# A two-layer network of fp32 products on one core: the three products of a chunk in another order, and a dozen small moves around the stages' seams

## The chip, the cores and the metric

The kernel runs on one core of one Trainium2 chip. The time is the device time of one execution in microseconds; a kernel's time is the median of its runs. TensorE is called PE here, its weight loads PEld, VectorE DVE, ScalarE ACT, GpSimd POOL, and the queue that issues most transfers SP.

## The reference, cut to what matters

Two blocks of a network of depth 2 each run after one another on x, 256 tokens of 1024 features, all in fp32. Cut to its shape:

```
for layer in 0, 1:                                    # first block
    x = x + 0.5 * swiglu(rms(x)) ;  x = x + mixer(rms(x))      # even: banded + stick-breaking attention; odd: dilated attention
    x = x + cross_attention(rms(x), rms(mem)) ; x = x + 0.5 * swiglu(rms(x))
for l in 0, 1:                                        # second block
    x = x + 0.5 * rms(swiglu(rms(x)))
    z = rms(x) @ w_in[l]                              # differential attention and an mLSTM read parts of z
    x = x + rms((g_a * (ya @ w_proj_a[l]) + g_m * (ym @ w_proj_m[l])) @ w_out[l])
    x = x + 0.5 * rms(swiglu(rms(x)))
swiglu(h) = (silu(h @ w_gate) * (h @ w_up)) @ w_down  # 1024 -> 2816 -> 1024
```

## The kernel before

There are 14 stages in a row: ffn0, even, xa0, ffn1, ffn2, odd, xa1, ffn3, ffn4, mix0, ffn5, ffn6, mix1, ffn7. Activations are held transposed, as [128 partitions, 8 chunks of features, 256 tokens]. Each fp32 product is made of three fp32r matmuls: with `w = w_hi + w_lo` and `a = hi + lo`, a chunk adds w_hi·hi, w_hi·lo and w_lo·hi. The weights come as 829 tiles of 512 KB: SP's queue loads one into `raw`, ACT casts it to `w_hi` (L1122), DVE subtracts to `w_lo` (L1558), and PE reads it from a ring of 6 slots (`RING`). A `w_tile` is 8 chunks by three matmuls of 256 columns, weights stationary, with the activations `a` or `b` moving; `down` and `tail_part` have the same three lines. A value tile (`v_half`) is the other way round: activations stationary, weights moving, and the order there is hi by w_hi, lo by w_hi, hi by w_lo. All matmuls are recorded at L476, the helper `mm`, except transposes (L879). Every third `w_tile` has a first matmul of 258 columns (`BESIDE`).

The order of work around the matmuls is written out by hand in lists of units, which each engine reads with its own part of a unit: `before(kind, layer)` stands ahead of a stage's attention, `between(kind, layer)` in it, `lstm_between(h, layer)` between the eight heads of the mLSTM. The units that the change touches are:

- `("mem",)`: ACT squares the memory's eight chunks (L1153), POOL adds them up (L2220); `("stat", "m")` is PE's sum over partitions of what POOL made.
- `vh(i, half)`: half of value tile i. `hs`, `hn`, `hb` are the three steps of a head norm: squares; their sum on PE, root on ACT (L1328) and reciprocal on DVE (L1847, then L1848, L1849); and the spread of the reciprocals over the heads by PE (`head_spread`, a matmul of 32 rows each) with DVE's products (L1873).
- `spread("diff", ...)` is such an `hb` of four matmuls and four L1873. It takes one of the two banks that `w_tile` writes in turn. DVE empties the bank of a `w_tile` at L1785.
- The stick-breaking attention (in the even stage) holds a softplus on ACT, which loads a table, between two rounds of PE.
- `post_norm` adds a normed stage to x: `temp = x * rt` is made by DVE for chunk 0 and by POOL for chunks 1 to 7 (L2335), DVE adds (L1667) and splits off the next stage's low part (L1585).
- `keep_going(n)` is n matmuls of no use, which PE runs while it waits.

The lines of a chunk in `w_tile`:

```
mm(out[:, 0:T], wh, hi[:, c, :], c == 0, False)
mm(out[:, 0:T], wh, lo[:, c, :], False, False)
last = mm(out[:, 0:T], wl, hi[:, c, :], False, c == C - 1)
```

Of the kernel before, what the change touches and what calls it, by code (L numbers as in the profile page):

```python
# [144 lines left out]
def build(nc, stream_d, x_d, mem_d, vec_d, con_d, biasa_d, biasc_d, heads_d, out_d, stages=STAGES):  # L145
    total = sum(TILES[s] for s, _ in stages)
    with ExitStack() as ctx:
# [106 lines left out]
        x_scaled = sem("x_scaled")  # L254
# [73 lines left out]
        def value_width(kind, i):  # L328
            return P if kind == "even" and i == 2 else T

        def before(kind, layer):
# [14 lines left out]
            def vh(i, half):  # L346
                return ("vh", "a" if kind == "odd" or kind == "even" else "b", "x" if kind in ("odd", "even") else "m", v, i, half, value_width(kind, i))
            if kind == "even":
                return [start(0, 1, 2), w(3, 0), hs("evq", 0, 0, 1), w(4, 1), ("col", "x"), hn("evq", 0, 0, 1),
                        hs("evq", 1, 2, 3), vh(0, 0), hn("evq", 1, 2, 3), hs("evk", 0, 4, 4), vh(0, 1), hn("evk", 0, 4, 4),  # L350
                        ("mem",), vh(1, 0), hb("evq", (0, 0, 1), (1, 2, 3)), vh(1, 1), hb("evk", (0, 4, 4)), ("stat", "m"),
                        vh(2, 0), ("col", "m"), ("att",), vh(2, 1)]
            if kind == "odd":
# [3 lines left out]
                def k(i):  # L357
# [4 lines left out]
                        w(13), hn(*q(3)), w(14), hs(*k(2)), w(15), hb("odq", q(2)[1:], q(3)[1:]), hs(*k(3)), hn(*k(2)), vh(0, 0)]  # L362
# [16 lines left out]
        def between(kind, layer):  # L379
# [3 lines left out]
            if kind == "odd":  # L383
                out = [[("vh", "a", "x", v, (g + 1) // 2, (g + 1) % 2, T)] for g in range(7)] + [[]]
                out[0].insert(0, ("hn", "odk", 3, layer, 14, 15))
                out[1].insert(0, ("hb", "odk", layer, ((2, 12, 13), (3, 14, 15))))
                return out
            if kind == "xa":
                k3 = ("xak", 3, layer, 6, 7)
                return [[("vh", "b", "m", v, 0, 1, T), ("hn", *k3)]] + [[("v", "b", "m", v, g)] for g in range(1, 4)]  # L390
# [4 lines left out]
        def lstm_between(h, layer):  # L395
# [6 lines left out]
            def spread(name, i, first):  # L402
# [4 lines left out]
                    2: [w0, spread("diff", 0, 0), w1],  # L407
                    3: [diff("hn", 2), w0, ("split", 0), ("split", 1), diff("hn", 3), w1],
                    4: [w0, spread("diff", 2, 4), long("hs", 0), w1],
# [46 lines left out]
        def _(pe):  # L456
# [25 lines left out]
            def w_tile(n, slot, out, hi, lo, ready=None, beside=0):  # L482

                wait_split(n)
                for c in range(C):
# [7 lines left out]
                    mm(out[:, 0:T], wh, lo[:, c, :], False, False)  # L493
                    last = mm(out[:, 0:T], wl, hi[:, c, :], False, c == C - 1)
# [58 lines left out]
            def v_half(buf, half, width=T):  # L553
# [9 lines left out]
                for e in range(4):  # L563
                    c = 4 * half + e
                    wh, wl = w_hi[:, slot, e * T:e * T + width], w_lo[:, slot, e * T:e * T + width]
                    for b in range(2):
                        o, tok = out[:, b * T:b * T + width], slice(b * P, b * P + P)
# [69 lines left out]
            def ffn(k, after_mixer):  # L637
# [44 lines left out]
                def down(n, slot, jj, J, first=False):  # L682
# [4 lines left out]
                    for c in range(C):  # L687
# [3 lines left out]
                        mm(out, wh, h[1][:, jj, :], False, False, True)  # L691
                        last = mm(out, wl, h[0][:, jj, :], False, False, True)
# [20 lines left out]
                if k >= 4:  # L713
                    sum_of_parts()
                    keep_going(4 if k < 7 else 0)
                t.next(x_ready, C)

            def unit(kind, *u):
# [15 lines left out]
                elif kind == "vh":  # L734
                    v_half(u[0], u[4], u[5])
# [17 lines left out]
            def head_sums(name, i, layer, a, b):  # L753
# [4 lines left out]
                if wide:  # L758
# [8 lines left out]
                if wide:  # L767
                    last = mm(bank[STAT][:, 0:T], mat, s[:, 0, :], True, True)
# [160 lines left out]
            def stick():  # L929
# [19 lines left out]
                wgt = z[:, 37:49, :].rearrange("p a t -> p (a t)").rearrange("p (h n) -> p h n", h=8)  # L949
                for h in range(8):  # L950
# [14 lines left out]
            def lstm(layer):  # L965
# [5 lines left out]
                for b in range(2):  # L971
                    last = mm(bank[1][:, 8 * b:8 * b + 8], g[:, b * P:(b + 1) * P], ident[0:8, 0:8], True, True)
                last.then_inc(gcol_mm, 1)
                pe.wait_ge(gcol_ready, t.next(gcol_ready))
# [21 lines left out]
                for h in range(8):  # L996
# [21 lines left out]
            def tail_part(tile, hi, lo, c0, c1):  # L1018
# [7 lines left out]
                for c in range(c0, c1):  # L1026
                    wh, wl = w_hi[:, slot, c * P:(c + 1) * P], w_lo[:, slot, c * P:(c + 1) * P]
                    mm(out[:, 0:T], wh, hi[:, c, :], c == 0, False)
                    mm(out[:, 0:T], wh, lo[:, c, :], False, False)
                    last = mm(out[:, 0:T], wl, hi[:, c, :], False, c == C - 1)  # L1030
# [3 lines left out]
            def mixer(kind, layer):  # L1034
# [45 lines left out]
                keep_going(4)  # L1080
# [16 lines left out]
        def _(act):  # L1097
# [75 lines left out]
            def ffn(k, following, after_mixer):  # L1173
# [25 lines left out]
                split_to(n0 + 6)  # L1199
# [1266 lines left out]
```

## Time and profile before

| what | before |
|---|---|
| runs | 2562.25, 2558.66, 2561.38 us, median 2561.38 |
| the profiled execution, its span | 2564.16 us, 2562.4 us |
| busy: PE, PEld, DVE, ACT, POOL | 2519.6, 2450.0, 1809.1, 1392.1, 241.0 us |
| matmuls, weight loads | 21289, 21289 |
| transfers | 446.43 MB, mean 174 GB/s |
| PE's granted clock, mean of the span | 0.992 |
| PE busy of the span's stretch: even (196 to 333) | 128.64 of 137 us, clock 0.93 |
| odd (795 to 900) | 102.82 of 105 us, clock 0.97 |
| mix0 (1386 to 1705), mix1 (2060 to 2381) | 314.20 of 319, 316.17 of 321 us |
| the eight ffn stretches, matmuls | 1633, 1720, 1719, 1708, 1678, 1596, 1490, 1488, together 13032 |

### The profile page before, as it was taken

To read this page: it belongs to the slowest core of one execution; us is meant where nothing else is said; L and a number is where in the kernel's file an instruction comes from. 1 tells how busy PE (TensorE), PEld (TensorE's weight loads), DVE (VectorE), ACT (ScalarE), POOL (GpSimd) and SP (SyncE) were. 2 spreads that over 40 slices of the span, in tenths; PEclk is the share of its full clock that TensorE was granted. 3 is DMA by queue.
4 is the path that set the end of the run, shared out by engine and by line. 5 is a ranking of instruction groups with operands and counts; after the bars stand their busy time and mean duration, and the time that the engine had idled before them with its cause. 6 is when DMAs were issued, how large, how long until landed. Compare 5 with 4: busy or idle time off the path is not lost.

```text
span 2562.4 us, 56110 instructions
## 1 busy us (share of the span) xinstructions
PE 2519.6 (98%) x21289; PEld 2450.0 (96%) x21289; DVE 1809.1 (71%) x2880; ACT 1392.1 (54%) x2228; POOL 241.0 (9%) x321
## 2 busy tenths in 40 slices
PE   9999999999999999999999999999999999999998
PEld 8998799999999899999999998999999999989998
DVE  7667586667667596767767767887676686687765
ACT  5445566445445766545445555654464465565543
POOL 1002011000000211000000070000000005301000
PEclk9998999999999999999999999999999999999999
DMA  7663245765655354565654543456555555435553
GB/s 268 213 198 127 96 151 159 237 209 186 200 196 172 100 175 143 193 196 172 213 190 162 191 157 120 162 171 194 192 176 193 189 164 175 139 121 177 182 195 115
DMA packets 123090, 446.43 MB, mean 174 GB/s; under 512 B 13696, under 2 KB 14848, under 8 KB 122944
## 3 DMA queue, kind: packets, MB, share of 16 engines
q1 hardware_dynamic: 120816, 436.79, 52.2%
q0 software_dynamic: 2128, 7.66, 0.9%
q8 instruction: 97, 1.59, 0.2%
q14 instruction: 49, 0.40, 0.0%
HBM read 443.34 MB, written 1.05 MB: 173 GB/s over the span
## 4 chain that ended last, share of the span: by engine, by line
PE 90%; DVE 7%; ACT 2%; issue 1%; POOL 0%; DMA 0%; SPq 0%; DVEq 0%; ACTq 0%; POOLq 0%
PE bank L476 89%; DVE w_lo L1558 2%; DVE rt L1853 1%; PE bank L879 1%; DVE z L1785 0%; DVE x L1667 0%; ACT w_hi L1122 0%; DVE rstd_x L1577 0%; DVE a L1585 0%; DVE score L1617 0%; DMA x<-in_x_dram 0%; ACT a L1143 0%; DVE score L1608 0%; DVE z L1857 0%; POOL score L2220 0%
## 5 line engine op out<-in xcount | busy, mean ns | idle before, releaser
L476 PE MATMUL bank<-a,w_hi 128*128 128x256 f32 x7472 | 1304.4, 279 | 9.9 <-ACT a L1143 4.2
L476 PEld LDWEIGHTS bank<-a,w_hi 128*128 128x128 f32 x7472 | 1132.1, 188 | 25.8 <-issue 14.4
L1558 DVE TENSOR_TENSOR w_lo<-raw,w_hi 128x1024 fp32r<-128x1024 f32 x829 | 1014.7, 1230 | 190.8 <-ACT w_hi L1122 185.4
L476 PE MATMUL bank<-a,w_lo 128*128 128x256 f32 x3736 | 1035.3, 277 | 0.0
L1122 ACT CAST w_hi<-raw 128x1024 fp32r<-128x1024 f32 x829 | 844.2, 1046 | 74.7 <-DMA raw<-in_stream_dram 51.9
L476 PE MATMUL bank<-b,w_hi 128*128 128x256 f32 (+1 forms) x4800 | 832.5, 277 | 1.2 <-DVE w_lo L1558 1.2
L476 PEld LDWEIGHTS bank<-b,w_hi 128*128 128x128 f32 x4800 | 723.9, 188 | 7.1 <-issue 3.1
L476 PEld LDWEIGHTS bank<-a,w_lo 128*128 128x128 f32 x3736 | 704.1, 188 | 0.0
L476 PE MATMUL bank<-b,w_lo 128*128 128x256 f32 x2400 | 663.5, 276 | 0.0
L476 PEld LDWEIGHTS bank<-b,w_lo 128*128 128x128 f32 x2400 | 450.9, 188 | 0.0
L1182 ACT CAST b<-hmid 128x256 fp32r<-128x256 f32 x132 | 53.7, 407 | 351.0 <-PE bank L476 335.5
L1178 ACT ACTIVATE sil<-sil 128x256 f32<-128x256 f32 x176 | 73.5, 417 | 167.2 <-DVE sil L1683 161.7
L1688 DVE TENSOR_TENSOR hmid<-bank,rstd_x 128x256 f32<-128x256 f32 x168 | 71.1, 423 | 126.3 <-PE bank L476 125.6
L1558 DVE TENSOR_TENSOR b<-hmid,b 128x256 fp32r<-128x256 f32 x132 | 56.0, 424 | 136.2 <-ACT b L1182 136.0
L476 PE MATMUL bank<-w_hi,a 128*128 128x256 f32 (+1 forms) x736 | 133.8, 285 | 0.0
L476 PEld LDWEIGHTS bank<-w_hi,a 128*128 128x128 f32 x736 | 114.7, 192 | 3.5 <-issue 2.4
L476 PE MATMUL bank<-w_lo,a 128*128 128x256 f32 (+1 forms) x368 | 103.9, 282 | 0.0
L2335 POOL TENSOR_TENSOR z<-x,rt 128x256 f32<-128x256 f32 x35 | 30.1, 894 | 642.4 <-ACT rt L1137 642.4
L1785 DVE TENSOR_TENSOR z<-bank,rstd_x 128x256 f32<-128x256 f32 x121 | 50.9, 421 | 55.8 <-PE bank L476 55.0
L1182 ACT CAST a<-hmid 128x256 fp32r<-128x256 f32 x44 | 17.9, 407 | 122.2 <-PE bank L476 117.5
L2204 POOL TENSOR_TENSOR score<-score 128x256 f32<-128x256 f32 x27 | 24.4, 903 | 610.4 <-ACT score L1153 609.6
L1702 DVE TENSOR_TENSOR hmid<-sil,hmid 128x256 f32<-128x256 f32 x176 | 74.8, 425 | 8.5 <-ACT sil L1178 0.7
(206 smaller groups left out, 1974.4 us busy)
## 6 DMA issues: line engine op xcount, KB each, us to landing
raw<-in_stream_dram SPq DMA_DIRECT2D x829, 512.0 KB, 3.8
z<-in_biasc_dram POOLq DMA_DIRECT2D x6, 512.0 KB, 4.6
z<-in_biasa_dram POOLq DMA_DIRECT2D x3, 512.0 KB, 4.9
x<-in_x_dram SPq DMA_DIRECT2D x2, 512.0 KB, 7.8
v<-in_mem_dram POOLq DMA_DIRECT2D x2, 512.0 KB, 7.0
out_dram<-x SPq DMA_DIRECT2D x8, 128.0 KB, 1.9
con<-in_con_dram POOLq DMA_DIRECT2D x1, 784.5 KB, 6.7
heads<-in_heads_dram POOLq DMA_DIRECT2D x1, 512.0 KB, 4.8
```

What stands on the lines that cost most here:

```text
L476: return nc.tensor.matmul(out, lhsT, rhs, start=start, stop=stop, skip_group_check=shared)
L879: last = nc.tensor.transpose(out[:, col:col + P], p[:, src:src + P], ident)
L1122: nc.scalar.copy(w_hi[:, slot, :], raw[:, raw_slot, :]).then_inc(hi_split, 1)
L1178: nc.scalar.activation(sil[:, jj, :], sil[:, jj, :], ACT.Silu).then_inc(silu_done, 1)
L1182: nc.scalar.copy(high_of["b"][:, to or jj, :], hmid[:, jj, :]).then_inc(hhi_done, 1)
L1558: return nc.vector.tensor_tensor(out, a, hi.bitcast(F32), ALU.subtract)
L1688: nc.vector.tensor_tensor(hmid[:, j % 2, :], gate_up_of(j, after_mixer)[1][:, 0:T], r, ALU.mult)\
L1702: nc.vector.tensor_tensor(hmid[:, jj, :], sil[:, jj, :], hmid[:, jj, :], ALU.mult)\
L1785: nc.vector.tensor_tensor(z[:, tile, :], out[:, 0:T], rstd[norm][:, :], ALU.mult).then_inc(w_evac, 1)
L1853: nc.vector.reciprocal(r, r).then_inc(hrecip, 1)
L2204: ins = nc.gpsimd.tensor_tensor(sq[:, 0, :], sq[:, 0, :], sq[:, c, :], ALU.add)
L2335: nc.gpsimd.tensor_tensor(z[:, 16 + c, :], x[:, c, :], rt[:, 0, 0:T], ALU.mult).then_inc(x_scaled, 1)
```

## The change

In `w_tile`, `down` and `tail_part` the second and third matmul of a chunk change places: high weights by high, low weights by high, high weights by low. `v_half` and the first chunks of a stage keep their orders. Beside it:

1. Even: `("mem",)` stands before the first value half; value tile 2 is computed in its full width of 256 (before: 128, the other half was of no use); 18 matmuls of no use of 128 columns stand in the stick-breaking attention before the second round, and DVE waits for them (`filled`) before its fourth output.
2. Odd: `hn(*k(3))` stands before the attention, not after its first exponentials.
3. Cross attention: the squares of `("xak", 3)` are added by a second matmul on PE instead of by POOL.
4. ffn 4 to 7: one `keep_going` matmul more ahead of `sum_of_parts()`, and 5 for 4 after it; mixers 5 for 4.
5. mLSTM: the columns of the gates go through another bank and PE waits for them later; `spread("diff", ...)` stands before w0 instead of after it at h = 2 and h = 4.
6. The mixers' `post_norm`: DVE makes all of `temp` itself.
7. Start of an ffn: DVE splits the first hidden tile before it does more scaling (`up_scale(1)`), and where x was rescaled ACT casts one more weight tile before the first silu.

```diff
@@ before(kind, layer)
             if kind == "even":
                 return [start(0, 1, 2), w(3, 0), hs("evq", 0, 0, 1), w(4, 1), ("col", "x"), hn("evq", 0, 0, 1),
-                        hs("evq", 1, 2, 3), vh(0, 0), hn("evq", 1, 2, 3), hs("evk", 0, 4, 4), vh(0, 1), hn("evk", 0, 4, 4),
-                        ("mem",), vh(1, 0), hb("evq", (0, 0, 1), (1, 2, 3)), vh(1, 1), hb("evk", (0, 4, 4)), ("stat", "m"),
+                        hs("evq", 1, 2, 3), ("mem",), vh(0, 0), hn("evq", 1, 2, 3), hs("evk", 0, 4, 4), vh(0, 1), hn("evk", 0, 4, 4),
+                        vh(1, 0), hb("evq", (0, 0, 1), (1, 2, 3)), vh(1, 1), hb("evk", (0, 4, 4)), ("stat", "m"),
                         vh(2, 0), ("col", "m"), ("att",), vh(2, 1)]
...
@@ lstm_between(h, layer)
-                    2: [w0, spread("diff", 0, 0), w1],
+                    2: [spread("diff", 0, 0), w0, w1],
...
@@ w_tile (down and tail_part alike)
-                    mm(out[:, 0:T], wh, lo[:, c, :], False, False)
-                    last = mm(out[:, 0:T], wl, hi[:, c, :], False, c == C - 1)
+                    mm(out[:, 0:T], wl, hi[:, c, :], False, False)
+                    last = mm(out[:, 0:T], wh, lo[:, c, :], False, c == C - 1)
...
@@ ffn, k >= 4
+                    keep_going(1)
                     sum_of_parts()
-                    keep_going(4 if k < 7 else 0)
+                    keep_going(5 if k < 7 else 0)
...
@@ head norm on PE
-                    last = mm(bank[STAT][:, 0:T], mat, s[:, 0, :], True, True)
+                    last = mm(bank[STAT][:, 0:T], mat, s[:, 0, :], True, added)
+                    if not added:
+                        last = mm(bank[STAT][:, 0:T], mat, s[:, 1, :], False, True)
...
@@ stick-breaking attention on PE
+                pe.wait_ge(bounded, t.next(bounded, 8) - 4)
+                for k in range(18):
+                    last = mm(bank[3][:, 384:512], ident, con[:, 0:P], False, False, True)
+                last.then_inc(filled, 1)
...
@@ lstm on PE
-                pe.wait_ge(gcol_ready, t.next(gcol_ready))
+                t.next(gcol_ready)
...
+                    if h == 0:
+                        pe.wait_ge(gcol_ready, t.so_far(gcol_ready))
...
@@ start of an ffn on ACT, then on DVE
-                split_to(n0 + 6)
+                split_to(n0 + 7 if rescaled[0] else n0 + 6)
...
-                up_scale(1, n0 + 3)
                 h_low(0, base)
                 split_to(n0 + 7)
+                up_scale(1, n0 + 3)
...
@@ post_norm on DVE; POOL's loop runs for stage "ffn" alone
+                def scaled(c):
+                    if c == 0 or not shared and c < C:
+                        chain(nc.vector.tensor_tensor(temp[:, c, :], x[:, c, :], rt[:, 0, 0:T], ALU.mult))
```

Three places as the engines' queues hold them. PE, in mix0 at h = 2, before: the end of w0 (`a` by the weights), the spread (`recip_two,spread_by`), the start of w1.

```order
L476 MATMUL bank<-a,w_lo 128x256
L476 MATMUL bank<-recip_two,spread_by 128x256 [waits w_evac,qk_ready,hrecip]
L476 MATMUL bank<-recip_two,spread_by 128x256
L476 MATMUL bank<-recip_two,spread_by 128x256 [waits h_bc]
L476 MATMUL bank<-recip_two,spread_by 128x256
L476 MATMUL bank<-a,w_hi 128x258 [waits lo_split,hi_split,w_evac]
L476 MATMUL bank<-a,w_hi 128x256
L476 MATMUL bank<-a,w_lo 128x256
```

The same place of the change: the spread, the start of w0 in the new order of a chunk (w_hi, w_lo, w_hi), and from its last matmul into w1.

```order
L472 MATMUL bank<-recip_two,spread_by 128x256 [waits h_bc]
L472 MATMUL bank<-recip_two,spread_by 128x256
L472 MATMUL bank<-a,w_hi 128x256 [waits lo_split,hi_split,w_evac]
L472 MATMUL bank<-a,w_lo 128x256
L472 MATMUL bank<-a,w_hi 128x256 x2
...
L472 MATMUL bank<-a,w_hi 128x256
L472 MATMUL bank<-a,w_hi 128x258 [waits lo_split,hi_split,qk_ready]
```

Now w1 waits for `qk_ready`, which is the last of the spread's four products on DVE, where it waited for `w_evac`, one L1785. In DVE's queue at this place, before:

```order
L2059 SCALAR_TENSOR_TENSOR v<-pt 128x256
L1785 TENSOR_TENSOR z<-bank,rstd_x 128x256 [waits tile_mm]
L1558 TENSOR_TENSOR w_lo<-raw,w_hi 128x1024 [waits hi_split]
L1873 SCALAR_TENSOR_TENSOR z<-z,vec,bank 128x256 [waits h_bc]
L1873 SCALAR_TENSOR_TENSOR z<-z,vec,bank 128x256 x3
```

and of the change, where L1883, L1795, L1563 and L2071 are before's L1873, L1785, L1558 and L2059:

```order
L2071 SCALAR_TENSOR_TENSOR v<-pt 128x256
L1883 SCALAR_TENSOR_TENSOR z<-z,vec,bank 128x256 [waits h_bc]
L1883 SCALAR_TENSOR_TENSOR z<-z,vec,bank 128x256 x3
L1795 TENSOR_TENSOR z<-bank,rstd_x 128x256 [waits tile_mm]
L1563 TENSOR_TENSOR w_lo<-raw,w_hi 128x1024 [waits hi_split]
```

The four products moved ahead of w0's L1785, and stand behind the head's own work (L2059) as before. In the odd stage DVE's queue reads before, after the first round of biases:

```order
L1558 TENSOR_TENSOR w_lo<-raw,w_hi 128x1024 [waits hi_split]
L1916 RECIPROCAL rr<-rs 128x4 [waits exp_done]
L1901 ISA score,nmx<-bank,z 128x128 [waits s_mm]
L1901 ISA nmx 128x1
L1901 ISA score,nmx<-bank,z 128x256
```

and with the change, where L1857 to L1859 are before's L1847 to L1849 (the reciprocals of `hn`), L1926 is L1916 and L1911 is L1901:

```order
L1563 TENSOR_TENSOR w_lo<-raw,w_hi 128x1024 [waits hi_split]
L1857 RECIPROCAL rt<-rt 128x256 [waits hroot]
L1858 CAST recip_two<-rt 128x256 [waits dve_step]
L1859 SCALAR_TENSOR_TENSOR recip_two<-recip_two,con,rt 128x256 [waits dve_step]
L1926 RECIPROCAL rr<-rs 128x4 [waits exp_done]
L1911 ISA score,nmx<-bank,z 128x128 [waits s_mm]
```

The three rows of `hn` moved from behind the second round of biases to ahead of L1916.

## Rows read from the trace of the kernel before

**Rows 1.** The page, busy time of each engine.

```profile
PE 2519.6 (98%) x21289; PEld 2450.0 (96%) x21289; DVE 1809.1 (71%) x2880; ACT 1392.1 (54%) x2228; POOL 241.0 (9%) x321
```

**Rows 2.** The page, costliest groups: count, busy us, mean ns of one, idle before.

```profile
L476 PE MATMUL bank<-a,w_hi 128*128 128x256 f32 x7472 | 1304.4, 279 | 9.9 <-ACT a L1143 4.2
...
L476 PE MATMUL bank<-a,w_lo 128*128 128x256 f32 x3736 | 1035.3, 277 | 0.0
...
L476 PE MATMUL bank<-b,w_hi 128*128 128x256 f32 (+1 forms) x4800 | 832.5, 277 | 1.2 <-DVE w_lo L1558 1.2
...
L476 PE MATMUL bank<-b,w_lo 128*128 128x256 f32 x2400 | 663.5, 276 | 0.0
```

**Rows 3.** PE's waits: releaser, us in total, times, longest.

```profile
PE bank L476 <- DVE a L1585: 3.5, 5, 1.1
...
PE bank L476 <- DVE z L1785: 2.2, 2, 1.1
...
PE bank L476 <- DVE w_lo L1558: 1.2, 3, 0.4
...
PE bank L476 <- ACT gcol L1431: 0.5, 2, 0.3
```

**Rows 4.** Timeline of the even stage around the memory's squares (ACT, POOL, PE).

```profile
210.54 1.05 ACT L1122 CAST w_hi<-raw 128x1024 fp32r<-128x1024 f32 x1 [2.06 <-DMA raw<-in_stream_dram]
...
216.85 7.61 POOL L2220 TENSOR_TENSOR score<-score 128x256 f32<-128x256 f32 x7 [22.20 <-ACT score L1153]
...
222.89 0.35 PE L476 MATMUL bank<-recip_two,spread_by 32*128 32x256 f32 x1 [0.59 <-DVE z L1873]
224.61 0.67 PE L476 MATMUL bank<-score,con 128*128 128x256 f32 x2 [1.37 <-POOL score L2220]
```

**Rows 5.** Windows: stretch, its us, busy of PE, PEld, DVE, ACT, POOL (x), clock, DMA share, GB/s.

```profile
226.46:240.12 13.66, 13.66 (x65) 12.11 (x65) 6.85 (x22) 6.13 (x19) 1.63 (x4) 0.50 0.26 87
284.49:291.32 6.83, 4.95 (x11) 3.13 (x12) 3.80 (x8) 5.97 (x8) 0.00 (x0) 0.50 0.00 0
...
2260.81:2264.22 3.41, 3.41 (x19) 3.19 (x17) 1.50 (x4) 0.00 (x0) 0.00 (x0) 0.50 0.49 154
```

**Rows 6.** Timeline, PE, the second round of the stick-breaking attention.

```profile
281.09 0.92 PE L476 MATMUL bank<-z 64*128 64x256 f32 x4
286.37 1.65 PE L476 MATMUL bank<-z,con 128*128 128x384 f32 x2 [4.36 <-DVE z L1973]
```

**Rows 7.** Timeline of the odd stage: DVE and PE around the second round of biases.

```profile
852.13 1.75 DVE L1847 RECIPROCAL rt<-rt 128x256 f32<-128x256 f32 x1 [3.17 <-ACT rt L1328]
...
854.29 0.67 PE L879 MATMUL bank<-con,score 128*128 128x128 f32 x3 [1.79 <-ACT pt L1366]
```

**Rows 8.** Timeline, DVE, mix0 at h = 4.

```profile
1584.52 0.41 DVE L2059 SCALAR_TENSOR_TENSOR v<-pt 128x256 f32<-128x256 f32 x1
1584.85 0.42 DVE L1785 TENSOR_TENSOR z<-bank,rstd_x 128x256 f32<-128x256 f32 x1
...
1586.31 1.65 DVE L1873 SCALAR_TENSOR_TENSOR z<-z,vec,bank 128x256 f32<-128x256 f32 x4
```

**Rows 9.** Timeline, PE: third and last matmul of two weight tiles and of a value half.

```profile
819.33 0.28 PE L476 MATMUL bank<-b,w_lo 128*128 128x256 f32 x1
...
821.71 0.28 PE L476 MATMUL bank<-b,w_lo 128*128 128x256 f32 x1
...
813.17 0.28 PE L476 MATMUL bank<-b,w_lo 128*128 128x256 f32 x1
...
815.64 0.28 PE L476 MATMUL bank<-b,w_lo 128*128 128x256 f32 x1
...
212.19 0.28 PE L476 MATMUL bank<-w_lo,a 128*128 128x256 f32 x1
...
214.67 0.28 PE L476 MATMUL bank<-w_lo,a 128*128 128x256 f32 x1
```

**Rows 10.** Windows, as rows 5: value tiles that follow a weight tile without a gap.

```profile
1439.00:1460.00 21.00, 21.00 (x187) 21.00 (x186) 11.34 (x13) 9.34 (x13) 0.28 (x1) 1.00 0.64 212
```

More of the change, by code:

```diff
@@ L383, in between @@
             if kind == "odd":
-                out = [[("vh", "a", "x", v, (g + 1) // 2, (g + 1) % 2, T)] for g in range(7)] + [[]]
-                out[0].insert(0, ("hn", "odk", 3, layer, 14, 15))
+                out = [[("vh", "a", "x", v, (g + 1) // 2, (g + 1) % 2)] for g in range(7)] + [[]]
                 out[1].insert(0, ("hb", "odk", layer, ((2, 12, 13), (3, 14, 15))))
@@ L389, in between @@
                 k3 = ("xak", 3, layer, 6, 7)
-                return [[("vh", "b", "m", v, 0, 1, T), ("hn", *k3)]] + [[("v", "b", "m", v, g)] for g in range(1, 4)]
+                return [[("vh", "b", "m", v, 0, 1), ("hn", *k3)]] + [[("v", "b", "m", v, g)] for g in range(1, 4)]
             rest = [("w", "a", "x", 16 + k) for k in range(8)] + [("v", "a", "x", v2, i) for i in range(4)]
@@ L551, in w_next, with v_half @@
                 at[0] += 1
-            def v_half(buf, half, width=T):
+            def v_half(buf, half):
                 if half == 0:
@@ L564, in v_half @@
                     c = 4 * half + e
-                    wh, wl = w_hi[:, slot, e * T:e * T + width], w_lo[:, slot, e * T:e * T + width]
+                    wh, wl = w_hi[:, slot, e * T:(e + 1) * T], w_lo[:, slot, e * T:(e + 1) * T]
                     for b in range(2):
-                        o, tok = out[:, b * T:b * T + width], slice(b * P, b * P + P)
+                        o, tok = out[:, b * T:(b + 1) * T], slice(b * P, b * P + P)
                         mm(o, hi[:, c, tok], wh, c == 0 and b == 0, False, True)
@@ L690, in down @@
                         mm(out, wh, h[0][:, jj, :], first and c % 2 == 0, False, True)
-                        mm(out, wh, h[1][:, jj, :], False, False, True)
-                        last = mm(out, wl, h[0][:, jj, :], False, False, True)
+                        mm(out, wl, h[0][:, jj, :], False, False, True)
+                        last = mm(out, wh, h[1][:, jj, :], False, False, True)
                     last.then_inc(tile_mm, 1)
@@ L757, in head_sums @@
                 t.next(hsq)
-                if wide:
+                added = wide and (name, i) != ("xak", 3)
+                if added:
                     pe.wait_ge(wide_added, t.next(wide_added))
@@ L1028, in tail_part @@
                     mm(out[:, 0:T], wh, hi[:, c, :], c == 0, False)
-                    mm(out[:, 0:T], wh, lo[:, c, :], False, False)
-                    last = mm(out[:, 0:T], wl, hi[:, c, :], False, c == C - 1)
+                    mm(out[:, 0:T], wl, hi[:, c, :], False, False)
+                    last = mm(out[:, 0:T], wh, lo[:, c, :], False, c == C - 1)
                 if c1 == C:
@@ L1079, in mixer @@
                 sum_of_all()
-                keep_going(4)
+                keep_going(5)
                 t.next(x_ready, C)
@@ L1257, in unit @@
                     out = bank[W_BANKS[turn[0] % 2]]
-                    width = u[5] if kind == "vh" else T
                     for b in range(2):
-                        nc.scalar.activation(dst[:, b, T * i:T * i + width], out[:, b * T:b * T + width], ACT.Copy,
+                        nc.scalar.activation(dst[:, b, T * i:T * i + T], out[:, b * T:(b + 1) * T], ACT.Copy,
                                              scale=rcol[norm][:, b:b + 1]).then_inc(v_ready, 1)
@@ L1656, in last_norm, with post_norm @@
                         add(c - 1)
-            def post_norm(source, name, following):
+            def post_norm(source, name, following, shared):
                 t.next(sq_made, C)
@@ L1760, in ffn @@
                     if following:
-                        post_norm(acc, f"post{k}", following)
+                        post_norm(acc, f"post{k}", following, True)
                     else:
@@ L2333, in _ @@
                     pool.wait_ge(root_ready, t.next(root_ready))
-                    for c in range(1, C if following else 0):
+                    for c in range(1, C if following and stage == "ffn" else 0):
                         nc.gpsimd.tensor_tensor(z[:, 16 + c, :], x[:, c, :], rt[:, 0, 0:T], ALU.mult).then_inc(x_scaled, 1)
```

27 lines of the change are left out of this document (14 added, 13 removed).

## The prediction, made blind

> **What bounds the kernel now.** I read the page's busy times first: PE is busy for 2519.6 of 2562.4 us and has 21289 matmuls, DVE 71%, ACT 54% [rows 1]. So PE sets the end, and a change can gain in three ways only: fewer waits of PE, a higher clock, or a shorter time from the start of one matmul to the start of the next. The waits come next, and are few and small: the longest kinds that this change touches are listed with their totals, 3.5, 2.2, 1.2 and 0.5 us [rows 3]. The clock stands at its lower level in a few stretches, of 13.66, 6.83 and 3.41 us among others [rows 5]. Last the pace, from starts in the timeline, since the mean of one (279 ns) overlaps with the next [rows 2]. In one weight tile 21 matmuls take 821.71 - 819.33 = 2.38 us, 113.3 ns each. In another of the same form, in the same stage, 815.64 - 813.17 = 2.47 us, 117.6 ns each, and in a value half 214.67 - 212.19 = 2.48 us, 118 ns [rows 9]. So PE has two paces at the same full clock, 4.4 ns apart. This is small for one matmul, but the product order is changed for nearly all of the 7472 + 3736 + 4800 + 2400 = 18408 matmuls of weight tiles [rows 2]: 18408 by 4.4 ns is 81 us, more than all other edits together.
>
> **The change part by part.** The sum is made against the profiled execution, 2564.16 us, of which 2562.4 is the span; it is 2.8 us above the median of the runs, 2561.38.
>
> *The memory's squares, even stage.* PE waits 1.37 us for POOL's adds (7.61 us, begun at 216.85) and 0.59 us just before for DVE [rows 4]. In the new place ACT does the squares in its idle 2.06 us ahead of the cast at 210.54, POOL begins near 209 and ends near 217, before PE is there: both waits go, -1.9 (bounds -1.4 and -2.0). What this uncovers is the clock: 2 us after these waits it falls for 13.66 us, in which 65 matmuls start [rows 5]; at full clock 65 would take 65 by 0.115 = 7.5 us. With the waits gone I expect the fall gone: -6.2. If the attention's small matmuls cause it, 0. Value tile 2 in full width is 48 matmuls, now 256 wide; the nearest rows say up to 118 ns [rows 9], and the narrow ones can't be below 106 if the load paces them: +0.2 (0 to +0.6).
>
> *Stick-breaking filler.* PE idles 4.36 us, then runs at the lower clock: of 6.83 us 4.95 are busy with 11 matmuls [rows 5, 6]. 18 matmuls of no use at about 0.11 us are 2.0 us and end near 284.0, ahead of the start at 286.37, so they cost nothing, and DVE's fourth output, which now waits for them, comes later than that. 2.4 us of idle time stay. If the clock stays up, 4.95 becomes 2.5: -2.5; if not, 0. Nothing in the trace decides: -1.2.
>
> *Odd stage.* The three reciprocal steps (1.75 us and two short ones, 2.5 together) now stand ahead of the second round of biases on DVE. PE's wait of 1.79 us is behind ACT, which in turn saves table loads; I put pt's copy 1.3 us later (0 to +2.0) [rows 7]. What is queued behind it on PE is the transpose and then the rest of the attention: +1.3.
>
> *Cross attention.* One more matmul on PE takes the place of a POOL add, in a stretch where PE waits anyway: 0 (to +0.4).
>
> *More keep_going.* Six more fp32 matmuls, some hidden by the root they wait for: +0.3 (0 to +2).
>
> *Gate columns.* The wait, 0.5 us in two, goes [rows 3]: -0.5.
>
> *Spreads before w0, twice in each of two mixers.* This is where the change adds a wait. Before, w1 waits at h = 4 only for one L1785, whose end is 1585.27. Now it waits for all four L1873 (1.65 us), and these can't begin before the head's own work, whose last operation L2059 ends at 1584.93 [rows 8]: 1584.93 + 1.65 = 1586.58, so w1 starts 1.28 us later. Behind w1 stands the next head's work, whose input ACT and DVE have ready by then, so nothing gives the time back. At h = 2 w1 had no wait, and the same sum gives +1.2. Four places: +5.0 (bounds +2, if DVE is ahead at h = 2, and +6). The idle time of PE at h = 4 grows from 1.1 to some 2.4 us; in mix1 the clock fell there already for 3.41 us with 19 matmuls (at full clock 2.2) [rows 5]. One more such fall costs 1.2, and a longer one more: +0.8.
>
> *post_norm.* PE's first chunk comes some 1 us earlier, and DVE's own products then hold back the later ones; of the 3.5 us of waits for L1585 [rows 3] little goes: -0.2 (-2 to +1).
>
> *Start of an ffn.* The first `down` waits for a low split behind `up_scale(1)`, 1.2 us in three places [rows 3]; the split is now ahead of it: -1.2 (0 to -1.2).
>
> *The order of products.* Every matmul has a weight load of its own, 21289 of each [rows 1], so the old order, which has w_hi twice in a row, saves no load, and the new one adds none. By the count of instructions it is worth 0. The pace is another matter. The value halves have had what is the new order's structure all along: the stationary operand changes at every matmul, the moving one stands twice. Where one follows a weight tile without a gap it keeps the fast pace: 21.0 us hold 187 matmuls with both edges counted, 185 by 113.5 ns [rows 10]. Where one starts after other work it has the slow pace and keeps it to its end, as at 212.19 [rows 9]; by my reading of the timeline this holds for all 23 such starts. Weight tiles after other work go back to the fast pace within five matmuls in 74 of 109 cases, as at 819.33, and stay slow in 35, as at 813.17 [rows 9]. So either the order decides whether PE finds back (then the change costs), or it is that weights move in a value half, and the order is nothing. I take 0.
>
> The Trainium skill, "TensorE: Matmul & The Clock Gate", Part 2, step ①, says that weights typically stay put across many matmuls, so that one load serves several; a reader would expect the old order to profit and this change to lose a load per chunk. The trace has one load for each matmul [rows 1], so this does not hold here. The same page, "LDWEIGHTS (loading the stationary operand)", gives columns / 1.2, 107 ns for 128; it would put both orders at one pace bound by the load, near the 113.3 shown, and says nothing of the second pace.
>
> The sum: -1.9 -6.2 +0.2 -1.2 +1.3 +0 +0.3 -0.5 +5.0 +0.8 -0.2 -1.2 +0 = -3.6, so 2560.6 for a profiled execution like that of before, and 2561.38 - 3.6 = 2557.8 for the median.
>
> **The rivals.**
>
> *A. The order loses the fast pace.* One mechanism: with the stationary operand changed each time, a weight tile that starts after other work, or meets a matmul of 258 columns, doesn't find back to 113.3 ns. For it: all value halves. Against it: the run of 185 at the fast pace in that very structure. If only the stages with attention pay (18408 less the ffn stages' 13032 is 5400 matmuls), 5400 by 4.4 ns = +24, less 4 already slow: about +20, and the median is 2578. If the ffn stages pay too, up to +75, 2633. It decides (slower by over 0.2%) from some 2,000 matmuls on.
>
> *B. The order cures the slow pace.* The 35 slow starts hold some 1,900 of the weight tiles' matmuls, and a matmul of 258 columns loses some 19 ns beside its width. With 1,900 by 4.4 ns = 8.4 and part of the second: -10, and 2548. For it: the slow runs begin mostly at the wide matmul. Against it: nothing shows why this order should help.
>
> *C. The clock falls anyway in the even stage.* PE's small matmuls of the attention follow at once. Then -6.2 isn't there: +2.6, 2564, a time that can't be told from before.
>
> *D. The spreads don't cost,* because DVE gets to L1873 before PE has finished w0: -8.6, 2552.8. Against it: the head's work on DVE ends at 1584.93 whatever the order of the rest [rows 8].
>
> **How the numbers follow.** About 0.2% (5 us) is what a measurement of this kernel can tell from no change. The forecast as it stands, with C and D as its edges: 0.50 (C 0.12 and D 0.08 among them); its own range is 2552 to 2568. A: 0.30. B: 0.20. Faster: 0.15 from the first, 0.16 from B, 0.01 from A, 0.32. Slower: 0.04 from the first, 0.22 from A, 0.26. Same: the rest, 0.42. The range goes down to 2544 (B) and up to 2600, which takes in A's first form and leaves out its ffn form, about 0.12; below lie some 0.05.
>
> **What the changed kernel's profile would show.** Memory: no wait of PE for L2220, and a clock of 1.00 from 226 to 240. Filler: 18 matmuls near 282, then either two levels of clock. Odd: the wait for L1366 near 3 us. Spreads: four waits of PE for L1873 of 1.2 to 2.5 us, in place of two of 1.1 for L1785. Start of an ffn: no wait for L1558. Order: the x187 of 21.0 us and the matmuls of an ffn stretch (1720 in 197 us) as before; where A holds, the same ffn stretch is 3 to 4% longer, and 21 matmuls take 2.47 us instead of 2.38. The forecast is wrong above all if the pace moves: 1 ns on each matmul of the weight tiles is 18 us.

## The result, and the profile after

The changed kernel takes 2590.13 us (2586.24 to 2593.61, three runs) against 2561.38 before: ratio 1.0101, 95% interval 1.0079 to 1.0122. It is slower by 28.8 us, where -3.6 was forecast. In the profiled execution the span went from 2562.4 to 2588.3 us. The page of the changed kernel, busy time of each engine and the groups that answer to [rows 1, 2]:

```profile
span 2588.3 us, 56224 instructions
...
PE 2552.5 (99%) x21347; PEld 2483.0 (96%) x21347; DVE 1810.7 (70%) x2894; ACT 1389.4 (54%) x2226; POOL 225.7 (9%) x305
...
L472 PE MATMUL bank<-a,w_hi 128*128 128x256 f32 x7472 | 1348.1, 280 | 8.6 <-DVE z L1883 6.0
...
L472 PE MATMUL bank<-b,w_hi 128*128 128x256 f32 (+1 forms) x4800 | 867.6, 279 | 1.8 <-DVE w_lo L1563 1.6
```

Only 58 matmul records came in addition, and PE is busy for 33 us more. Its idle time in the span fell, from 42.8 to 35.8 us. So the loss is no wait: PE takes longer for nearly the same work. (The groups with `w_hi` show 79 us more of busy time, but this isn't the pace alone: in `after_old_at_wide` below, which has the new order nearly everywhere and doesn't lose, the two groups stand at 1335.8 and 855.8 us, 55 more than before. The order decides which matmuls of a group overlap.) The waits, with those of before in [rows 3]:

```profile
PE bank L472 <- DVE z L1883: 7.6, 5, 2.1
...
PE bank L879 <- ACT pt L1371: 3.7, 4, 2.2
...
PE bank L472 <- DVE a L1590: 2.4, 3, 1.2
...
PE bank L472 <- DVE w_lo L1563: 1.6, 2, 0.8
```

Windows of the changed kernel show where the time is (columns as in [rows 5]): two of 16 us in ffn1 to either side of a wide matmul (I call the matmuls of 258 columns that), then the two places of the even stage where the clock had fallen.

```profile
452.00:468.00 16.00, 16.00 (x138) 16.00 (x138) 10.38 (x14) 7.24 (x10) 0.00 (x0) 1.00 0.71 248
470.00:486.00 16.00, 16.00 (x143) 16.00 (x143) 10.38 (x14) 7.11 (x11) 0.53 (x1) 1.00 0.64 220
...
226.00:240.00 14.00, 14.00 (x120) 12.89 (x118) 8.25 (x25) 10.07 (x28) 1.63 (x4) 1.00 0.34 115
284.00:291.30 7.30, 7.30 (x54) 5.42 (x53) 1.54 (x4) 5.00 (x13) 0.00 (x0) 1.00 0.00 0
```

In the first of the first two windows 138 matmuls fall into 16 us (edges counted), in the second 143, at the same clock of 1.00 and with the same weight tiles: 117.8 and 113.3 ns from start to start. [rows 9] had shown both paces before. What is new is how they alternate. The timeline of PE around 451.60, the wide matmul ahead of the first of the two windows, cut to the matmuls with `w_lo`, one in three:

```profile
451.03 0.28 PE L472 MATMUL bank<-a,w_lo 128*128 128x256 f32 x1
...
451.37 0.28 PE L472 MATMUL bank<-a,w_lo 128*128 128x256 f32 x1
...
451.60 0.28 PE L472 MATMUL bank<-b,w_hi 128*128 128x258 f32 x1
...
452.07 0.28 PE L472 MATMUL bank<-b,w_lo 128*128 128x256 f32 x1
...
452.42 0.28 PE L472 MATMUL bank<-b,w_lo 128*128 128x256 f32 x1
```

Ahead of the wide matmul a `w_lo` comes 0.34 us after the other (three matmuls), behind it 0.35. From here to the end of ffn1 the intervals between starts are 143 at the slow pace (117.8 ns), a wide matmul, 3 longer ones and 141 at the fast pace (113.3 ns), a wide matmul, 143 at the slow pace, and so on. I sorted the intervals from each matmul of a weight tile (the wide ones left out) to the next matmul into fast (under 115 ns) and slow (115 to 126 ns) and summed what the latter are above 113.3. The last column is the same sum for the value tiles:

| trace | fast | slow | above 113.3 ns | value tiles' |
|---|---|---|---|---|
| before | 16005 | 2047 | 10.0 us | 4.3 us |
| changed | 8609 | 9455 | 42.6 us | 5.4 us |

That is 32.6 and 1.1, together +33.7 us. "Without the pace" below means that a stage's part of these sums is taken off. With both traces cut at the same matmuls, the even stage takes 8.3 us less (8.7 without the pace), mix0 4.9 and mix1 0.6 us more (2.7 more and 0.6 less without it), and ffn0 is 1.9 us shorter without it. With some 0.7 us for the rest that makes the span's 25.9. (ffn0's share looks like chance: without the pace it lies between 2.5 us less and 0.7 more in the other 14 traces, also where nothing in it was changed.)

### The profile page after: what moved, and what is told of

It is laid out like the page before. It is cut to its first block, busy times and chain, and to the rows that moved or that the text cites. A ratio compares the mean times of both kernels' runs of the same rounds, so it can differ in the third digit from the quotient of the medians.

```text
span 2588.3 us, 56224 instructions
## 1 busy us (share of the span) xinstructions
PE 2552.5 (99%) x21347; PEld 2483.0 (96%) x21347; DVE 1810.7 (70%) x2894; ACT 1389.4 (54%) x2226; POOL 225.7 (9%) x305
## 4 chain that ended last, share of the span: by engine, by line
PE 90%; DVE 8%; ACT 1%; issue 1%; DMA 0%; POOL 0%; SPq 0%; DVEq 0%; ACTq 0%
PE bank L472 89%; DVE w_lo L1563 2%; DVE rt L1863 1%; PE bank L879 1%; DVE z L1795 0%; DVE rt L1857 0%; DMA raw<-in_stream_dram 0%; ACT w_hi L1128 0%; DVE rstd_x L1582 0%; DVE z L1883 0%; DVE x L1676 0%; ACT score L1359 0%; DVE z L1867 0%; DVE a L1590 0%; DVE z L1671 0%
## 5 line engine op out<-in xcount | busy, mean ns | idle before, releaser
L472 PE MATMUL bank<-a,w_hi 128*128 128x256 f32 x7472 | 1348.1, 280 | 8.6 <-DVE z L1883 6.0
L472 PEld LDWEIGHTS bank<-a,w_hi 128*128 128x128 f32 x7472 | 1157.2, 189 | 25.0 <-issue 10.2
L1563 DVE TENSOR_TENSOR w_lo<-raw,w_hi 128x1024 fp32r<-128x1024 f32 x829 | 1016.2, 1232 | 197.6 <-ACT w_hi L1128 194.0
L472 PE MATMUL bank<-b,w_hi 128*128 128x256 f32 (+1 forms) x4800 | 867.6, 279 | 1.8 <-DVE w_lo L1563 1.6
L472 PEld LDWEIGHTS bank<-b,w_hi 128*128 128x128 f32 x4800 | 745.1, 189 | 7.4 <-issue 3.6
L1563 DVE TENSOR_TENSOR b<-hmid,b 128x256 fp32r<-128x256 f32 x132 | 56.0, 425 | 142.1 <-ACT b L1188 141.2
L472 PE MATMUL bank<-w_hi,a 128*128 128x256 f32 x736 | 131.6, 281 | 0.0
L472 PE MATMUL bank<-w_lo,a 128*128 128x256 f32 x368 | 102.5, 278 | 0.0
L1795 DVE TENSOR_TENSOR z<-bank,rstd_x 128x256 f32<-128x256 f32 x121 | 51.0, 422 | 59.7 <-PE bank L472 58.7
L1693 DVE TENSOR_TENSOR sil<-bank,rstd_x 128x256 f32<-128x256 f32 x160 | 67.6, 422 | 15.2 <-PE bank L472 11.2
```

The source lines that it names most:

```text
L472: return nc.tensor.matmul(out, lhsT, rhs, start=start, stop=stop, skip_group_check=shared)
L1563: return nc.vector.tensor_tensor(out, a, hi.bitcast(F32), ALU.subtract)
L1693: nc.vector.tensor_tensor(sil[:, j % 2, :], gate_up_of(j, after_mixer)[0][:, 0:T], r, ALU.mult)\
L1795: nc.vector.tensor_tensor(z[:, tile, :], out[:, 0:T], rstd[norm][:, :], ALU.mult).then_inc(w_evac, 1)
```

## The experiments

Ratios are to the kernel before on the same chip, whose median there was 2564.06, 2567.81, 2564.16 and 2564.24 us in the four sets of runs. "Slow" with a number is the count of the table above in the profiled run.

**Is it the order?** The kernel before with the new order alone (the lines of `w_tile`; `down` and `tail_part` alike):

```diff
-                    mm(out[:, 0:T], wh, lo[:, c, :], False, False)
-                    last = mm(out[:, 0:T], wl, hi[:, c, :], False, c == C - 1)
+                    mm(out[:, 0:T], wl, hi[:, c, :], False, False)
+                    last = mm(out[:, 0:T], wh, lo[:, c, :], False, c == C - 1)
```

> The kernel before with the new order of the three products in w_tile, down and tail_part, and nothing else. Theory T (toggle): with the new order each matmul of 258 columns flips PE between its two paces (113.3 and 117.8 ns), so about half of the weight tiles' matmuls are slow: +33 us, 2594 (2588 to 2600), and the matmuls at 117 ns or more come up from 2,000 to about 9,500. Theory S (seams): the loss of the whole change comes from the moved steps, the order is worth 0: 2561.

2600.38 us, ratio 1.0136 (1.0115 to 1.0158), 9590 slow matmuls. It is the order, and alone it costs more than the whole change.

The changed kernel with the old order (the diff above reversed):

> The changed kernel with the old order of the products. Theory T: 2553 to 2557, faster than before by 0.2 to 0.3%, because the moved steps alone give -8 in the even stage and +2 to +3 in the mixers. Theory S: about 2588, as the change.

2568.84, ratio 1.0012 (1.0000 to 1.0025), 4810 slow: the loss is gone, the expected gain isn't there. Windows of ffn5 and ffn6 in its trace say why:

```profile
1700.00:1850.00 150.00, 148.99 (x1313) 148.82 (x1313) 105.26 (x148) 72.17 (x98) 0.00 (x0) 1.00 0.61 200
1890.00:2040.00 150.00, 150.00 (x1275) 150.00 (x1274) 100.39 (x138) 68.63 (x92) 0.00 (x0) 1.00 0.59 195
```

ffn6 is slow from its first tile to its last (1439 of 1439 intervals, ten wide matmuls among them), and so is ffn7: 6.3 and 6.2 us. Single runs lie anywhere from 2562 to 2573. So a stage can begin at the slow pace and keep it for its whole length, in the old order too, and each such stage costs 6.2 to 6.3 us. Neither theory had counted on this.

**What do the wide matmuls do?** `BESIDE = 2` became `BESIDE = 0`, in the changed kernel and in that of before.

> The changed kernel, new order, without the wide matmuls (258 columns become 256). Theory T: nothing flips the pace, so a run of tiles keeps what it begins with; most begin fast, so about 2553 (2545 to 2565), and the ffn stretches have 113.3 ns throughout. Rival P: the new order can't hold the fast pace whatever the widths, or locks the runs that begin slow for good: 2590 or more, up to 2630 where long ffn runs begin slow.

2565.64, ratio 1.0018 (1.0005 to 1.0030), 3893 slow: with the new order and no wide matmul the ffn stages keep the pace they begin with, seven fast and ffn5 slow throughout. The new order can hold the fast pace.

> The kernel before, old order, without the wide matmuls. Theory T: in the old order PE goes back to the fast pace by itself after a wide matmul, so these cost 167 by about 27 ns, and without them the time is 2557 (-4). Rival W: the wide matmuls are what brings slow runs back to the fast pace, and without them the slow ones stay slow to the end of their run: 2565 to 2600.

2575.55, ratio 1.0053 (1.0034 to 1.0072), 3833 slow: here the rival was right in part. In the old order a wide matmul often ends a short stretch at 117.8 ns, and without them ffn6 was slow throughout, and the mixers lost 3.3 us more to the slow pace than in the kernel before.

The changed kernel with two wide matmuls, in chunks 0 and 1:

```diff
-                    if beside and c == 0:
-                        mm(out[:, 0:T + beside], wh, both_of[id(hi)][:, c, 0:T + beside], True, False)
+                    if beside and c < 2:
+                        mm(out[:, 0:T + beside], wh, both_of[id(hi)][:, c, 0:T + beside], c == 0, False)
```

> The changed kernel, new order, with two wide matmuls (258 columns) in a tile that has one now, in its chunks 0 and 1. Theory T (each wide matmul flips the pace): the second flips back what the first flipped, so runs keep the pace they began with but for three matmuls: 2565 (2557 to 2575), and the slow matmuls come down from 9,500 to 2,500 to 5,000. Rival K: a wide matmul brings in the slow pace and something else brings back the fast one: 2590 or more.

2584.12, ratio 1.0070 (1.0046 to 1.0094), 7456 slow. Both numbers of theory T missed, but what it said of the pairs held: of the wide matmuls 106 stood in slow work and left it slow, 147 in fast work and left it fast, and 6 went from slow to fast. The time is lost because ffn0, ffn1 and ffn3 began slow and stayed so (1566 to 1571 intervals of 1583).

**Which operand?** The kernel before with a third order in all chunks (the lines of `w_tile`, cut; `down` and `tail_part` alike):

```diff
-                        mm(out[:, 0:T], wh, hi[:, c, :], c == 0, False)
-                    mm(out[:, 0:T], wh, lo[:, c, :], False, False)
-                    last = mm(out[:, 0:T], wl, hi[:, c, :], False, c == C - 1)
+                        mm(out[:, 0:T], wl, hi[:, c, :], c == 0, False)
+                    mm(out[:, 0:T], wh, hi[:, c, :], False, False)
+                    last = mm(out[:, 0:T], wh, lo[:, c, :], False, c == C - 1)
```

> The kernel before with a third order of the same three products: low weights by high, high by high, high weights by low (the wide matmul is the first, so it loads w_lo). It has both pairs: the moving operand twice (as the new order) and the stationary one twice (as the old). If the moving pair is what lets a wide matmul throw PE into the slow pace: +30, about 2594. If the stationary pair is what brings PE back: 2564, as before.

2595.20, ratio 1.0100 (1.0072 to 1.0128), 9788 slow: it flips like the new order, though `w_hi` stands twice in a row again. A pair of equal weights doesn't protect.

**Near or everywhere?** Two kernels cross the orders: in the changed kernel only the chunk with a wide matmul has the old order (its line is shown), in the kernel before only that chunk has the new one (the same line with the two pairs exchanged).

```diff
+                    for x, y, end in (((wh, lo, False), (wl, hi, True)) if beside and c == 0 else ((wl, hi, False), (wh, lo, True))):
+                        last = mm(out[:, 0:T], x, y[:, c, :], False, end and c == C - 1)
```

> The changed kernel with the new order everywhere but in the chunk that holds the wide matmul (chunk 0 of some w_tiles, 167 chunks of about 6,000), which has the old order. Theory N (near): it is the matmul behind the wide one that decides: with the same moving operand again (high, high) it flips the pace, with another (high, low) it doesn't. Then 2565 to 2572, with 2,000 to 5,000 slow matmuls. Theory G (general): the order of all the others decides: 2590, with 9,500 slow ones.

2563.18, ratio 0.9993 (0.9981 to 1.0005), 3593 slow, ffn5 throughout.

> The kernel before with the old order everywhere but in the chunk that holds the wide matmul, which has the new one. Theory N: these 167 chunks alone bring the whole loss of the order: 2597 (+30), about 9,500 slow matmuls. Theory G: 2565, as before.

2598.66, ratio 1.0137 (1.0118 to 1.0156), 9775 slow. 167 chunks carry the whole loss. Windows of 160 us, of ffn2 of this kernel and of ffn1 of the one ahead of it:

```profile
630.00:790.00 160.00, 160.00 (x1385) 160.00 (x1384) 104.12 (x144) 74.72 (x103) 0.00 (x0) 1.00 0.61 197
```

```profile
435.00:595.00 160.00, 160.00 (x1412) 160.00 (x1412) 107.34 (x148) 76.32 (x104) 2.63 (x5) 1.00 0.66 218
```

In the old order the matmul behind the wide one has the same stationary and another moving operand, in the new one another stationary and the same moving one. In this kernel both change, in the wide chunks alone (w_lo·hi wide, w_hi·lo, w_hi·hi):

```diff
-                        mm(out[:, 0:T + beside], wh, both_of[id(hi)][:, c, 0:T + beside], True, False)
+                        mm(out[:, 0:T + beside], wl, both_of[id(hi)][:, c, 0:T + beside], True, False)
...
+                    for x, y, end in (((wh, lo, False), (wh, hi, True)) if beside and c == 0 else ((wh, lo, False), (wl, hi, True))):
```

> The kernel before with the old order everywhere but in the chunk that holds the wide matmul: there low weights by high (the wide one), then high weights by low, then high by high. The matmul behind the wide one has another stationary and another moving operand. If what flips the pace is the same moving operand again (theory M): no flips, about 2564 as before. If it is that the stationary operand changes behind the wide one (theory C; in the old order it is the same w_hi): flips as with the new order, 2598, about 9,700 slow matmuls.

2563.68, ratio 0.9999 (0.9988 to 1.0011), 2039 slow. The same window of ffn2 as above holds 1412 matmuls here for 1385 there:

```profile
630.00:790.00 160.00, 160.00 (x1412) 160.00 (x1411) 105.87 (x144) 76.49 (x103) 0.00 (x0) 1.00 0.62 204
```

That its wide matmul has `w_lo` as stationary operand is not what helps, since `before_both_pairs` has the same wide matmul and flips. So it is the moving operand: the same 256 columns right behind a matmul that read them and 2 more. One thing stays untested: in all eight traces without a flip behind 258 columns the neighbour reads `lo`, which lies next to `hi` (the 2 extra columns are its first ones), and no third operand was tried.

And `before_new_at_wide` with `BESIDE = 16`:

> The kernel of before_new_at_wide (the old order but for the chunks with the wide matmul, which have the new one) with a wide matmul of 272 columns in place of 258. If any matmul that is longer than the others flips the pace here: 2600, with about 9,700 slow ones. If the flip hangs on the 2 columns: another number of slow matmuls, somewhere from 2564 to 2610.

2570.85, ratio 1.0020 (1.0007 to 1.0033), 2287 slow, no wide matmul that turned fast work slow (118 left it fast). With 16 columns more there is no flip, so the flip hangs on the 2. The runs lie between 2562.9 and 2576.9; the profiled one (2566.06) has no stage that is slow throughout, and what the longer ones lose isn't shown.

**What are the other edits worth?** The kernel before with the memory's squares ahead and the 18 fillers (cut: `("mem",)` goes one line up, and DVE waits for the fillers as in the change):

```diff
-                        ("mem",), vh(1, 0), hb("evq", (0, 0, 1), (1, 2, 3)), vh(1, 1), hb("evk", (0, 4, 4)), ("stat", "m"),
+                        vh(1, 0), hb("evq", (0, 0, 1), (1, 2, 3)), vh(1, 1), hb("evk", (0, 4, 4)), ("stat", "m"),
...
+                pe.wait_ge(bounded, t.next(bounded, 8) - 4)
+                for k in range(18):
+                    last = mm(bank[3][:, 384:512], ident, con[:, 0:P], False, False, True)
```

> The kernel before with two of the even stage's edits alone: the memory's squares moved ahead of the first value half, and the 18 filler matmuls. They are worth the -8.7 us that the even stage shows in the changed kernel's trace: 2555.4 (2552 to 2559) beside 2564.1. Rival L: a slow ffn stage, +6.5 us each, comes or goes by chance and hides it: anything from 2553 to 2570 with runs in steps of some 6 us.

2558.90, ratio 0.9970 (0.9952 to 0.9987), 8.9 us less. In its trace the even stage is 9.0 us shorter than in the kernel before. Its twelve runs stand in three groups, five at 2552.8 to 2554.1, three at 2558.9 to 2560.4, four at 2562.6 to 2567.5.

The changed kernel with the old order and some edits undone: spreads and ffn's start; spreads alone; spreads and `hn(k3)` of the odd stage. The spreads' part of the edit:

```diff
-                    2: [spread("diff", 0, 0), w0, w1],
+                    2: [w0, spread("diff", 0, 0), w1],
...
-                    4: [spread("diff", 2, 4), w0, long("hs", 0), w1],
+                    4: [w0, spread("diff", 2, 4), long("hs", 0), w1],
```

> The changed kernel with the old order, the spreads back behind w0 and the start of an ffn as it was. From the traces: even stage -8.7, spreads' waits +3.8 and the start's +0.7 not paid: 2554 (2551 to 2558) where all ffn stages run at the fast pace, 6.5 more for each that doesn't. It is the candidate that beats both kernels.

2558.20, ratio 0.9961 (0.9945 to 0.9977); runs near 2551 (five), 2558.5 (five) and 2565 (two).

> The changed kernel with the old order and the spreads back behind w0; the ffn's start stays as changed. Beside the last such kernel, which had the ffn's start as before and waits of 1.15 us in ffn5 and ffn7, it should show 0.89: 0.5 us better, 2557.7 median, in steps of 6.5 from 2550. Rival: the start is worth nothing, or the slow stages come more often: 2558 to 2565.

2556.89, ratio 0.9970 (0.9953 to 0.9986); near 2550.5 (three), 2556.5 (four), 2562.8 (five).

> The same with hn(k3) of the odd stage back in the attention too. The odd stage of the changed kernels took 1.0 us more on average than that of the kernels with the old place (104.97 against 103.94), so 1 us less than the kernel above: fastest runs near 2549. Rival: the difference is that of the clock there and nothing changes.

2550.68, ratio 0.9957 (0.9942 to 0.9972), runs from 2547.9: the lowest median of all kernels here, below the kernel before and the changed one. Its odd stage takes 103.7 us for the 104.7 of the kernel ahead of it. The intervals of the last three overlap, and more of its runs stand at the lowest step, so how much of the 6 us between the last two medians is the edit (1 us by the trace) and how much luck is open.

## Why the prediction was wrong

**Order of products: the step that failed.** The text says "either the order decides whether PE finds back (then the change costs), or it is that weights move in a value half, and the order is nothing. I take 0." It is +33.7 us by the traces, and +36 when run alone. The value of 0 was a choice between two readings of the rows, and nothing in them decided it. The range up to 2600 holds 2590 only because it took in rival A; the forecast's own range ended at 2568. Rival A had the right sign and the right resource: order and pace. But its mechanism ("with the stationary operand changed each time ... doesn't find back") is refuted twice: a kernel that has the new order everywhere but behind the wide matmuls is as fast as before, and the kernel in which the stationary operand changes behind the wide matmul, but the moving one too, doesn't flip. What happens is a flip at each wide matmul whose columns are read again at once. In the four traces with that neighbour, two more columns and one wide matmul in a tile, 272 turned fast work slow, 247 slow work fast, and none left it as it was (counted where the nine intervals ahead of it and the tenth to eighteenth behind it can be told as fast or slow); in the eight with another neighbour 892 left fast work fast, none turned it slow. Hence the size, which lies between A's two forms: not the stages with attention alone and not everything, but every second stretch in all stages, half of the weight tiles' matmuls. The rows for it stood in the trace: each wide matmul in a stretch at 113.3 ns cost three longer intervals and then PE was back, and I priced the stretches at 117.8 ns but not what it would be if that return failed. With the 33.7 us taken off, the span fell by 7.8 us where the sum has -3.6; the parts follow.

**Rival B,** that the order cures the slow pace, is refuted. In the changed kernel a wide matmul ends a slow stretch, but begins the next.

**The even stage** was forecast at -9.1 with the filler and came to -8.7, but not from the parts that I gave; that the sums are close is luck. POOL's adds are no longer waited for, but PE then waits longer for L1883:

```profile
224.82 0.35 PE L472 MATMUL bank<-recip_two,spread_by 32*128 32x256 f32 x1 [1.59 <-DVE z L1883]
...
276.73 4.29 PE L472 MATMUL bank<-con 128*128 128x128 f32 x36
```

1.59 us are idle where 1.96 were [rows 4]: of -1.9, only -0.4 came. The clock gave more than I took: 1.00 in both windows above, where the filler was counted at half its possible 2.5. The filler itself was mis-sized. The second row is its 18 matmuls, each with two records: they take 4.29 us and not 2.0, and the second round starts at 281.16, 0.14 us behind them. So almost none of the idle 4.36 us of [rows 6] is left, where I had left 2.4. It fitted by chance: the round is no later than before (5.28 us from the start of the last `z` matmuls in both traces). Rival C is refuted.

**Odd stage.** The wait is 2.2 us for 1.79 [rows 7], and the stage takes 104.9 us on average in seven traces with the new place against 103.9 in nine with the old one: +0.9, forecast +1.3.

**Spreads.** PE waits for L1883 four times in the mixers, 0.9 us at h = 2 and 2.1 at h = 4, 6.0 in all, in place of 2.2 for L1785 [rows 3]: +3.8 of the +5.0. I had put 1.2 at h = 2 and 1.3 more at h = 4, where 0.9 and 1.0 came: the term was too large by 1.2 us in all.

With the spreads back, mix0 and mix1 are 2.6 and 3.9 us shorter than in the changed kernel with the old order, 6.5 together, so with the clock behind the waits the forecast's +5.8 was near (the former has one stretch of 3.4 us at the lower clock in mix1, the latter none). Rival D is refuted.

**More keep_going.** The change adds nine of these matmuls and not six, and each has two records, as the filler's have. Together with the filler (36 records) and the cross attention's (4) that makes the 58 of the page. No run shows their cost by itself.

**post_norm and the ffn's start** together were forecast at -1.4. At the end of mix0 PE waited twice in the kernel before (first two rows) and waits once in the changed one (third row):

```profile
1690.40 0.36 PE L476 MATMUL bank<-a,w_hi 128*128 128x256 f32 x1 [1.42 <-ACT a L1143]
...
1693.24 0.50 PE L476 MATMUL bank<-a,w_hi 128*128 128x256 f32 x2 [1.12 <-DVE a L1585]
```

```profile
1707.37 0.51 PE L472 MATMUL bank<-a,w_hi 128*128 128x256 f32 x2 [0.57 <-DVE a L1590]
```

From the last but one weight matmul of a mixer to the 73rd of the ffn behind it PE takes 14.1 to 14.2 us in all eight traces with the changed seam, 15.1 in the trace of the kernel before: 0.9 us at each of the two. But most of it is given back at once. The first `down` now waits 0.81 us for `w_lo` in ffn5 and ffn7, where it waited 0.44, and up to the 151st matmul of the ffn it is 24.8 us for 25.1: some 0.3 each. With the ffn's start as it was (`after_old_both_back`) that wait is 1.27 us and the stretch 25.0, so the new start gives some 0.25 of the 0.3, 0.5 us in the two, where -1.2 was forecast for it. The single worth of `post_norm` and of the `keep_going` matmul in this seam wasn't run apart.

These 0.3 us are what the pair of traces shows, and it shows too little. In seven of the eight traces of kernels with the old seam PE runs at the lower clock for 3.4 or 6.8 us at one or both of the mixers' ends, and the same stretch takes up to 27.0 us. The one without is the trace that the forecast was made from. None of the eight with the changed seam has such a fall. So the edits at this seam can give up to 2.2 us at each mixer, which neither the forecast nor the two profiled executions could show. The gate columns' wait is gone, as forecast.

## What to carry to other kernels

When PE is busy for 98% and its idle time doesn't grow, look at the distance between starts, sorted into levels, before anything else: 4.5 ns on some 7,400 more of the 18408 matmuls is 33 us, more than the whole result. A matmul of another width among equal ones is a disturbance; what stands right behind it can decide the pace of the next hundred, so an edit that reorders products has to be judged there and not by its count of instructions. And where single runs stand in steps (here some 6 us), a kernel needs many runs, and its trace shows only one of the steps. The same holds for the clock: the one trace before had no fall at the mixers' ends, and most of its kind have.

## What the runs showed of the hardware

PE has two paces for back-to-back fp32r matmuls of 256 columns with a load each, 113.3 and 117.8 ns, at the same granted clock, and stays in one for over 1,400 matmuls. Which one it takes at a start differs from stage to stage; that it differs from run to run too is inferred from the steps of some 6 us in the times, since each kernel has one trace. A matmul of 258 columns, followed by one on the same moving columns, changed the pace every time (519 of 519, four traces); followed by one on `lo` it never made it slow (892 of 892), and ended a stretch at 117.8 ns 89 times and left it 52 times (eight traces). With 272 columns, followed by the same moving columns, it left the fast pace alone in all of 118 cases (one trace). What the slow pace is inside PE, and why a wide matmul ends it in some places of the old order and not others, stays open. And a wait of 2.1 us with the same work around it was followed by 3.4 us at the lower clock or by none: in mix0 the granted clock was 0.89 from 1590 to 1606, in mix1 1.00 from 2276 to 2290, as the windows show:

```profile
1590.00:1606.00 16.00, 13.83 (x88) 12.36 (x87) 11.94 (x23) 4.35 (x8) 0.00 (x0) 0.89 0.30 100
2276.00:2290.00 14.00, 11.82 (x87) 10.62 (x86) 11.05 (x24) 4.59 (x8) 0.00 (x0) 1.00 0.29 99
```
